# A first stage's normed columns in rows of 576 columns that start on multiples of 256 bytes

## The reference

```
first block
  hn = rmsnorm(h);  z = hn @ w_in                     (projections: 29 tiles of 128 outputs)
  y  = [mlstm(z), forgetting_attention(z)];  h += y @ w_out
  x  = rmsnorm(h[:, 16:])
  q  = x @ peer_query                                 (16 half-heads of 128)
  top 16 x 16 product keys per head -> 128 experts of 16384 per token, gate = softmax
  h += sum_e gate_e * gelu(u_e . x) * v_e
second block
  h += 0.5 rmsnorm(swiglu(rmsnorm(h)));  h += rmsnorm(hybrid_mixer(rmsnorm(h)));  h += 0.5 rmsnorm(swiglu(rmsnorm(h)))
```

## The kernel before

| first byte, modulo 256 | before | after |
|---|---|---|
| `hn`, first kept column of channel c | 96 + 64 c: 96, 160, 224, 32, then again | 0 for every c |
| `hn`, second half of 264 columns | 64 + 64 c | 224 |
| `w_hi`, `w_lo`, every block of 128 columns | 32 | 224 |
| `units_hi`, `units_lo` | 32 | 224 |
| `y`, first kept column | 96 + 64 c | 32 + 64 c |
| tiles of the second block | as they are | the same |

## Time and profile before

### The profile page before, as it was taken

How to read it: one execution, slowest core, us unless ns; L and a number is a source line. 1 busy time by engine, 2 the same in 40 slices (tenths; PEclk the granted TensorE clock), 3 DMA queues, 4 the chain that set the end, 5 groups by cost and what they waited for, 6 DMA issues and landing times. The chain is left out here.

```text
span 3580.2 us, 52582 instructions
## 1 busy us (share of the span) xinstructions
PE 3500.5 (98%) x19484; PEld 2987.7 (83%) x19484; DVE 1772.8 (50%) x3403; ACT 1265.5 (35%) x1838; POOL 500.3 (14%) x428
## 2 busy tenths in 40 slices
PE   8999999999999999999999999999999999899999
PEld 8966787888888888888888899998889789768887
DVE  7344699566665224444444533335445456653333
ACT  4244322466665232222222322223223333333232
POOL 0000125433332001111111010010100000111011
PEclk9999999999999999999999999999999989999999
DMA  4200234355555546566666322222222100123221
GB/s 149 77 18 21 86 99 137 130 182 183 183 181 179 182 148 196 188 194 195 195 193 194 116 94 95 83 95 69 92 85 77 59 1 1 42 71 99 94 98 68
DMA packets 115449, 416.07 MB, mean 116 GB/s; under 512 B 14193, under 2 KB 14321, under 8 KB 113009
## 3 DMA queue, kind: packets, MB, share of 16 engines
q1 hardware_dynamic: 75632, 279.93, 23.9%
q0 software_dynamic: 18944, 67.12, 6.4%
q10 hardware_dynamic: 20736, 67.12, 5.0%
HBM read 344.91 MB, written 69.21 MB: 116 GB/s over the span
## 5 line engine op out<-in xcount | busy, mean ns | idle before, releaser
L447 DVE TENSOR_TENSOR w_lo<-ring,w_hi 128x1024 fp32r<-128x1024 f32 x224 | 274.6, 1226 | 707.8 <-ACT w_hi L443 707.8
L183 DVE TENSOR_TENSOR w_lo<-ring,w_hi 128x1024 fp32r<-128x1024 f32 (+2 forms) x157 | 205.9, 1311 | 567.1 <-ACT w_hi L177 567.1
L443 ACT ACTIVATE w_hi<-ring 128x1024 fp32r<-128x1024 f32 x255 | 270.4, 1060 | 507.0 <-PE ps L493 485.2
L463 PE MATMUL ps<-hn_hi,w_hi 128*128 128x512 f32 x1024 | 408.1, 399 | 3.4 <-POOL w_lo L447 2.2
L463 PE MATMUL ps<-hn_lo,w_hi 128*128 128x512 f32 x1024 | 404.5, 395 | 0.0
L463 PE MATMUL ps<-hn_hi,w_lo 128*128 128x512 f32 x1024 | 402.9, 393 | 0.0
L493 PE MATMUL ps<-units_lo,w_hi 128*128 128x512 f32 x1024 | 398.7, 389 | 0.0
L493 PE MATMUL ps<-units_hi,w_hi 128*128 128x512 f32 x1024 | 398.7, 389 | 0.0
L493 PE MATMUL ps<-units_hi,w_lo 128*128 128x512 f32 x1024 | 398.7, 389 | 0.0
L177 ACT ACTIVATE w_hi<-ring 128x1024 fp32r<-128x1024 f32 (+2 forms) x170 | 190.2, 1119 | 453.4 <-PE ps L241 379.8
L241 PE MATMUL ps<-f_hn_hi,w_hi 128*128 128x264 f32 (+1 forms) x1056 | 284.3, 323 | 8.9 <-DVE f_hn_lo L867 8.5
(11 more groups left out here) (431 smaller groups left out, 6697.0 us busy)
## 6 DMA issues: line engine op xcount, KB each, us to landing
ring<-in_w_uv SPq DMA_DIRECT2D x256, 512.0 KB, 3.4
ring<-in_f_up SPq DMA_DIRECT2D x88, 512.0 KB, 3.3
expert_units<-scratch ACTq DMA_DIRECT2D x128, 256.0 KB, 2.7
gate_table<-peer ACTq DMA_DIRECT2D x16, 2048.0 KB, 7.2
peer<-gate_table POOLq DMA_DIRECT2D x32, 1024.0 KB, 7.9
peer<-expert_units POOLq DMA_DIRECT2D x128, 256.0 KB, 3.7
ring<-in_w_in SPq DMA_DIRECT2D x29, 512.0 KB, 3.3
ring<-in_w_late SPq DMA_DIRECT2D x25, 512.0 KB, 3.3
```

The costliest lines, as they stand in the source:

```text
L183: self.nc.vector.tensor_tensor(self.l[:, self.slot(k), 0:self.cols], e.ring[:, self.ring(k), 0:self.cols], self.h[:, self.slot(k), 0:self. ...
L443: A_(uh[:, slot(n)], e.ring[:, ring(n), 0:D], ACT.Copy).then_inc(e.hi_done, 1)
L447: ops.tensor_tensor(ul[:, slot(n)], e.ring[:, ring(n), 0:D], uh[:, slot(n)].bitcast(F32), ALU.subtract).then_inc(e.lo_done, 1)
L463: mm = M(e.ps[:, n % 2, :], u[:, slot(n), ch * P:(ch + 1) * P], x[part][:, ch, META:L], start=(ch == 0 and j == 0), stop=(ch == DC - 1 and ...
```

## The change

The rows of `hn` become 576 columns long (2304 bytes, 9 x 256), of which the first 528 are used, and the tile begins so that column 16 lies on a multiple of 256 bytes. `front` is 160 bytes here. The region grows from 33,792 to 37,312 bytes, so all that is behind it moves by 3520 bytes. `attend` and the masks keep their addresses. No instruction is added or taken away.

```
+LINE = 64
+ROW = 9 * LINE
...
         with ExitStack() as outer:
-            shared = Region(nc, outer, "columns1", 2 * DC * tile_bytes)
-            hn = [shared.at(f"hn1_{x}", i * DC * tile_bytes, DC, L, dt=F32R) for i, x in enumerate(("hi", "lo"))]
+            rows_bytes = 4 * 2 * DC * ROW
+            shared = Region(nc, outer, "columns1", rows_bytes + 4 * (2 * LINE - META))
+            front = -(shared.base + 4 * META) % (4 * LINE)
+            hn = [shared.at(f"hn1_{x}", front + i * rows_bytes // 2, DC, ROW, dt=F32R)[:, :, 0:L]
+                  for i, x in enumerate(("hi", "lo"))]
```

## The result

The changed kernel takes 3586.49 us (median of 21 runs, 3580.93 to 3593.7), the kernel before 3580.94 (21 runs): ratio 1.0016, 95% interval 1.001 to 1.0022. It is slower by 0.16%. The prediction said 3537.5 us, 1.2% faster, and gave 10 in 100 to a change of less than 0.2%, where the measured one lies, and 9 in 100 to slower by more. The measured time lies above its range.

A forecast was written before the change was run, and what follows sets the result against it. TensorE was taken as the bound. From the median of 3581.9 us, 44.4 us were subtracted for 512-column matmuls on aligned `hn`, all other terms being 0, giving 3537.5 us; the likeliest case's range was 3528 to 3547.

The forecast's parts named there:

- What bounds the kernel: Whole kernel: TensorE busy 98% of the span, so in the affected stretches one nanosecond per matmul is one of the end.
- The distances now, 231.7 and 226.7 ns, and that addresses make them: Start-to-start spacing of 512-column matmuls before the change: 231.7 ns in line 463, 226.7 in line 493, set by addresses.
- The 5 ns follow the address: Lines 463 and 493: the 5 ns between them come from `hn` walking over four places while `units` stay at 32.
- What a start at a multiple of 64 costs: Line 463: aligned 512-column matmuls would take 218.3 ns, inferred from 264-column halves; 3312 x (231.7 - 218.3) = 44.4 us gained.
- Its bounds: An aligned 512-column matmul lies between 216.3 ns, from plain float32's 3 ns over its columns, and 226.7 ns, as line 493.
- The unit of 16 columns: Spacing counted in 6.67 ns units: misaligned starts cost 2 at place 32, 3 at the others; whole numbers supported it.
- Line 241, 0 with a bound of 2 us: Queries on `hn`: 600 pairs of 264-column matmuls lose only the walk; taken as 0, at most 2 us either way.
- Line 493, 0, by the difference: `units` and weights move together from 32 to 224, relative place unchanged: 0; 20.5 us lost if absolute place counts.
- The other engines' tiles keep their place modulo 64: ScalarE, VectorE, GpSimd and DMAs work on tiles with unchanged place modulo 64 and wait for TensorE: 0 on the path.
- What the faster stream runs into: Line 463 and queries: GpSimd, ScalarE and VectorE keep enough slack, top-k keeps 3 us, so the whole 44.4 us arrive.
- the walk alone: Rival, 0.13: only the walk costs 5 ns, alignment nothing; line 463 falls to 226.7 ns, 16.6 us gained, 3565 us.
- Slower: Rival, 0.09: `units` at 224 cost 20.5 us in line 493, `hn` gains nothing, 3602 us, or 16.6 us, 3586.

The follow-up runs named there:

- coarse sweep: TensorE-only kernel, computation left out: 64 streams of 512 float32r columns, columns and weights each at eight places in steps of 32 bytes; 226.7 to 234.4 ns a matmul.
- finer sweep: TensorE-only kernel, computation left out: column-weight differences in 8-byte steps, multiples of 256, fewer weight columns, 264-column halves; 226.7 ns at difference 0, 240.0 at 120.
- mended kernel: Changed kernel with one number of `front` altered: first kept column of `hn` at 224 modulo 256, where its weights lie; 3570.36 us, ratio 0.9967.
- all-at-32 kernel: Changed kernel with a 37,120-byte region returning weights to 32 modulo 256, and `hn`'s first kept column at 32 too; 3562.08 us, ratio 0.9955 to the kernel before.

## Why the prediction was wrong

- **What bounds the kernel**: right in the main. TensorE is the bound in these stretches, and the runs follow its distances, but for the first 32 tiles of line 465. Units 32 bytes from their weights cost 20.4 us in their stretch, 3072 distances of 6.67 ns.
- **The distances now, 231.7 and 226.7 ns, and that addresses make them**: right, and reproduced by TensorE alone.
- **"The 5 ns follow the address ... the columns of `units` always begin at 32"**: half right. All weights of the kernel lay at 32, so the trace of before could not tell place 32 from difference 0, as the prediction itself said of `units`. It then used the first reading for `hn` and the second for `units`. One reading had to serve both. With the difference taken seriously, `hn` at 0 beside weights at 224 is a new difference of 32, which no row showed, and its price was open in both directions.
- **"What a start at a multiple of 64 costs"**: the step that failed. It split the surcharge into a part for the start and a part for the end, and gave what the 264-column halves lacked to their aligned starts. The sweeps show no such worth of an aligned start: at 512 columns no aligned stream takes less than 226.7 ns, and at 264 columns, with weights at 0, the starts at 0, 64, 128 and 192 take 120.0, 121.0, 123.3 and 120.7 ns, those at 32, 96, 160 and 224 take 122.1, 121.7, 121.7 and 120.0. Streams of 264 columns pay 10.0 to 13.3 ns over their columns wherever they start, less than most streams of 512; why is open. What stood in its place is the difference of the places: `hn` at 0 beside weights at 224 takes 233.3 ns, not 218.3. The 44.4 us that hung on this step became a loss of 3312 x 1.6 = 5.3 us; line 465 and the queries show 5.4. The reading under it was of an exceptional tile as well: with the 244.7 ns a pair of the rest of the stage, its own sum gives 219.7 ns instead of 218.3.
- **Its bounds**: the four plain float32 "matmuls" of the earlier trace rows are the records of two. The 3 ns over 426.7 are right for a record (429.2 ns), but no float32r stream of 512 columns comes nearer to its columns than 13.3 ns. The section of the Trainium skill that is named there ("Back-to-back issue gap") calls N / 2.4 + 2.5 ns the gap of an isolated matmul and says nothing of addresses.
- **The unit of 16 columns**: 34 and 35 units are what the coarse sweep shows at difference 0 and at most others. The nine matmuls of 35 each are not: by the table the dear places of the walk are 34.3, 35 and 35. The finer sweep has 230.0 and 231.7 ns as well, 34.5 and 34.75 units, so whole numbers were no evidence.
- **Line 241, 0 with a bound of 2 us**: the pairs take 240.0 ns. Against the 243.3 of the earlier trace rows that is 600 x 3.3 = 2.0 us gained, against 244.7 it is 2.8; the stretch shows 1.1.
- **Line 493, 0, by the difference**: right, and shown three ways (unchanged after the move, unchanged in the mended kernel, 6.67 ns dearer once set apart). The reason given there, uneven spacing within a channel, was a hint at the right theory, and I should have carried it over to `hn`.
- **The other engines' tiles keep their place modulo 64**: not `hn` itself, which they write and whose kept columns go from 32 to 0. It cost nothing that shows: ScalarE's busy time is 1265.6 us (1265.5 before), VectorE's 1757.1 (1772.8 before).
- **What the faster stream runs into**: not tested by the change, since line 465 did not get faster. In the all-at-32 kernel half of the gain in the first 32 tiles does not arrive, 1.9 us of 3.7, and TensorE's waits there go from 3.5 to 4.7 us, all for GpSimd. "The whole 44.4 us arrive" would not have held for those tiles. The top-k kept its room, 16.8 us of the 17.2.
- **The rivals**: "the walk alone" predicted 226.7 ns for any constant place and fell. "Slower" named the wrong line: `hn` gained nothing, but `units` paid nothing. Its other number, 3586 us, is the measured one by luck: it sets a loss of 20.5 us at `units` against a gain of 16.6 at `hn`, and neither came. The sign came from a difference worse than the average of the walk, which no rival had. The Trainium skill's 16-byte lines (SBUF — State Buffer, "Specifications (TRN2)") would, as the prediction applied them, have all starts at multiples of 32 bytes equal; the coarse sweep has nothing but such starts and runs from 226.7 to 234.4 ns, so here the measurement decides against it.

Open: why the difference counts. The pattern shows in float32r alone of the three types and repeats every 256 bytes. Every stream here loads weights before each matmul, so whether it needs a load beside it was not tested. The 10.9 ns over bfloat16 that stay at difference 0 are not explained either, nor why the same code at the same addresses can run at two steady levels: the pairs of the second block's first feed-forward stage take 244.7 ns before and 243.3 in the all-at-32 kernel, which does not touch them.

## What to carry to other kernels

Before giving an aligned address a price, list every address that moves at the same time and every one that stays: if all operands of one kind sit at one place, the trace can't tell a place from a difference, and the price of a new pair is unknown in both directions. For streams of 512-column float32r matmuls put the moving columns and the stationary weights at the same place modulo 256 bytes, and make the row length a multiple of 256 bytes. That was worth 2 to 3% of such a matmul here. For other lengths measure first: 256 columns were cheaper at a difference of 32. For plain float32 and bfloat16 it was worth nothing.

## What the runs showed of the hardware

- A stream of 512-column float32r matmuls takes 226.7 ns each when columns and weights start at the same place modulo 256 bytes, 228.8 when the columns are 64 bytes further, 232.4 to 234.4 at the other multiples of 32, and 240.0 at 120. Absolute place, bank order of PSUM and the distance between rows (multiples of 256) have no effect. A difference of 48 took 230.0 ns in one kernel of streams and 233.3 in another.
- At 256 columns a difference of 0 takes 120.0 ns and one of 32 takes 116.7. What a matmul takes over its columns at difference 0 runs from 10.0 ns (264 columns) to 20.0 (448).
- The same code at the same addresses ran its pairs of 264 columns at 244.7 ns in one kernel and at 243.3 in another.
- For 512 columns a plain float32 matmul takes two records of 429.2 ns each and a bfloat16 one 215.8 ns, at every one of eight differences.
- Fewer columns of weights do not shorten a float32r stream at difference 0: 226.7 ns with 128, 230.0 with 96, 229.9 with 64 and 231.7 with 32, though the loads go from 188 ns to 161, 134 and 109.
